# The mixer's linears take x times its weight, with 1/rms applied where VectorE reads them out

## The reference, cut to what matters

```python
xn = rms_norm(h, ln1_g)                 # x / sqrt(mean(x*x) + 1e-6) * gain
proj = xn @ w_in                        # columns: u_s5, q, k, v, gate_logits
gates = sigmoid(gate_logits + b_gate)   # g_s5, g_attn
y_s5 = s5_mixer(u_s5, ...) @ w_s5_branch
y_attn = sliding_window_attention(rms_norm(q), rms_norm(k), v, ...) @ w_attn_branch
h = h + (g_s5 * y_s5 + g_attn * y_attn) @ w_out
h = h + peer_mixer(rms_norm(h, ln2_g), ...)
```

## Time and profile before

| | us |
|---|---|
| median of 3 runs | 4320.23 |
| lowest and highest | 4318.43, 4323.8 |
| the profiled execution | 4325.75 |
| its span, first to last instruction | 4323.9 |

### The profile page before, as it was taken

One profiled execution on the slowest core, in us unless ns is written; L12 is line 12 of the kernel. 1 busy time (PEld: TensorE's weight loads), 2 busy tenths in 40 slices (PEclk: granted clock), 3 DMA queues, 4 the chain that ended last, 5 costly groups with the idle time before them and its releaser, 6 DMA issues.

```text
span 4323.9 us, 50161 instructions
## 1 busy us (share of the span) xinstructions
PE 3998.2 (92%) x15912; PEld 2782.1 (64%) x15912; DVE 2172.7 (50%) x4235; ACT 1290.0 (30%) x2792; POOL 2264.6 (52%) x2979
## 2 busy tenths in 40 slices
PE   8999987778777777999999999999999999999998
PEld 6777633333333333688867767888888867768887
DVE  8466786776777775432154544331332165534322
ACT  2132322222222222422223433332332133323222
POOL 6655633333333333566655445665665745536664
PEclk9999999999999999999999999999999999999999
DMA  6331699999999999423222112323223212213232
GB/s 161 85 113 67 261 427 427 427 427 427 425 427 427 414 427 427 162 95 97 93 71 71 62 62 79 106 96 99 94 97 95 97 55 69 78 46 109 95 96 82
DMA packets 182757, 807.79 MB, mean 187 GB/s; under 512 B 40544, under 2 KB 45072, under 8 KB 117008
## 3 DMA queue, kind: packets, MB, share of 16 engines
q0 software_dynamic: 73728, 536.90, 29.5%
q1 hardware_dynamic: 79936, 256.76, 18.1%
q10 hardware_dynamic: 28880, 11.54, 1.4%
HBM read 796.87 MB, written 7.34 MB: 186 GB/s over the span
## 4 chain that ended last, share of the span: by engine, by line
PE 62%; DMA 15%; DVE 9%; issue 5%; POOL 5%; ACT 2%; DVEq 1%; ACTq 0%; POOLq 0%; SPq 0%
PE bank L771 16%; PE bank L773 15%; PE bank L772 15%; DMA rows_w<-in_peer_uv,expert 5%; PE bank L1176 5%; DMA rows_o<-in_peer_uv,expert 5%; POOL wl L644 5%; DMA rows_x<-in_peer_uv,expert 3%; DMA work<-in_peer_uv,expert 1%; DVE rows_w L2403 1%; PE bank L860 1%; DVE rows_o L2403 1%; DVE rows_x L2403 1%; PE bank L1217 1%; PE bank L1349 1%
## 5 line engine op out<-in xcount | busy, mean ns | idle before, releaser
L644 POOL TENSOR_TENSOR wl<-raw,wh 128x256 fp32r<-128x256 f32 (+1 forms) x1928 | 1515.1, 815 | 645.4 <-ACT wh L1744 605.3
L771 PE MATMUL bank<-xh,wh 128*128 128x512 f32 x2304 | 918.7, 399 | 3.5 <-POOL wl L644 1.9
L773 PE MATMUL bank<-xh,wl 128*128 128x512 f32 x2304 | 900.4, 391 | 0.0
L772 PE MATMUL bank<-xl,wh 128*128 128x512 f32 x2304 | 899.2, 390 | 0.0
L771 PEld LDWEIGHTS bank<-xh,wh 128*128 128x128 f32 x2304 | 433.6, 188 | 133.3 <-issue 35.8
L1744 ACT ACTIVATE wh<-raw 128x1024 fp32r<-128x1024 f32 x296 | 312.2, 1056 | 693.3 <-PE bank L773 570.0
L773 PEld LDWEIGHTS bank<-xh,wl 128*128 128x128 f32 x2304 | 433.6, 188 | 92.4
L772 PEld LDWEIGHTS bank<-xl,wh 128*128 128x128 f32 x2304 | 434.2, 188 | 87.2 <-issue 1.9
L2449 DVE TENSOR_TENSOR work<-bank,rstd 128x512 f32<-128x512 f32 x176 | 121.3, 691 | 537.8 <-PE bank L773 536.3
L1176 PE MATMUL bank<-rows_w,diag 128*128 128x512 f32 x624 | 314.0, 653 | 82.1 <-ACT diag L1708 82.1
L1176 PE MATMUL bank<-rows_o,diag 128*128 128x512 f32 x640 | 308.1, 630 | 69.2 <-ACT diag L1708 69.2
(11 more groups left out here) (473 smaller groups left out, 6015.0 us busy)
## 6 DMA issues: line engine op xcount, KB each, us to landing
raw<-in_w_l SPq DMA_DIRECT2D x316, 512.0 KB, 3.2
raw<-in_w_l SPq DMA_DIRECT2D x64, 448.0 KB, 3.3
raw<-in_w SPq DMA_DIRECT2D x54, 512.0 KB, 3.2
raw<-in_w_l SPq DMA_DIRECT2D x56, 256.0 KB, 2.6
raw<-in_w SPq DMA_DIRECT2D x20, 256.0 KB, 2.6
bias_scratch<-work ACTq DMA_DIRECT2D x1, 3072.0 KB, 33.1
raw<-in_uq_l SPq DMA_DIRECT2D x8, 384.0 KB, 3.0
rows_o<-in_peer_uv,expert POOLq DMA_INDIRECT x160, 19.5
```

The lines of the kernel that those rows point to most:

```text
L644: last = gp.tensor_tensor(wl[:, slot, c], raw[:, rslot, c], f32(wh[:, slot, c]), ALU.subtract)
L771: pe.matmul(bank[b][:], wh[:, slot, c], ah, start=k == 0, stop=False)
L772: pe.matmul(bank[b][:], wh[:, slot, c], al, start=False, stop=False)
L773: mm = pe.matmul(bank[b][:], wl[:, slot, c], ah, start=False, stop=k == last)
```

## The change

- x is no longer normalised before the linears. ACT writes `xh` = round(x * gain) straight from x, DVE writes `xl` = x * gain - xh, and neither waits for `rstd`.
- The squares use three buffers. PE adds four before linear u0 and four behind it; ACT then makes `rstd`, which stays in its tile until the end of the attention.
- 1/rms is applied when a linear is read: by DVE, as bank * rstd, for u (four), k, v (two each), gate_s and gate_a (eight each), where ACT read them before. ACT's tanh then works on the stored tile. q is read unscaled by ACT; its own norm takes eps * rms * rms as epsilon instead (`q_eps`, from four small PE products of `rstd`), and its square root is four instructions instead of one.
- SP loads the second half of x behind the first weight tile.
- The phase tables come from two ACT sines over 128x1024 of an angle that DVE makes in five instructions, in place of the doublings and widenings.
- On DVE the powers of C stand before the turned inputs and the scan. The readouts of k stand before the scan, those of v and gate_s behind the states.
- On PE the lag matrices stand two to a k-step within q3 (i = 3), and wait for one copy of the turned powers rather than eight; the second four turns follow q3; `steps_in` runs whole after i = 5. On ACT the eight `u_step` loads and the bias DMA stand behind q1's readout, where they stood behind q0's.
- In the attention ACT copies the odd transpose between the exps of its two items, not after both.

```diff
 
 
-TURN_AFTER, LAGS_WITH, IN_WITH, OUT_WITH = (2, 3), (4, 5), 6, (15, 16, 17)
+TURN_AFTER, LAGS_WITH, IN_AFTER, SHIFT_AFTER, OUT_WITH = (2, 3), 3, 5, (5, 6), (15, 16, 17)
 
...
             sp.dma_start(c1[:], d["cols1"]).then_inc(c1_loaded, 16)
-            for n in range(2):
+
+            def load_x(n):
+
                 half = slice(n * KD // 2, (n + 1) * KD // 2)
                 sp.dma_start(x[:, half, :], d["xT"].rearrange("(k p) t -> p k t", p=P)[:, half, :]).then_inc(x_loaded[n], 16)
...
-
+                        if stage == "u" and j == 0:
+                            load_x(1)
+
+            load_x(0)
             stage1("u", "w8_1")
...
-            norm(KD, None)
-            ready = normed_ready()
-            first_two(AT_1["u"], None, ready)
-            for j in range(2, 4):
+            def add_square(k):
+
+                pe.wait_ge(sq_ready.sem, sq_ready.at(use.next("sq"), None))
+                mm = pe.matmul(total[:], ones[:], square_tile[k % 3], start=k == 0, stop=k == KD - 1)
+                mm.then_inc((sq_used if k < KD - 1 else summed).sem, 1)
+
+            wait_total(None)
+            for k in range(4):
+                add_square(k)
+            linear(AT_1["u"], 0, None, normed, normed_ready())
+            for k in range(4, KD):
+                add_square(k)
+            for j in range(1, 4):
                 linear(AT_1["u"], j, None, normed)
...
-            pe.matmul(turn[0:HEADS1, 0:3 * P], tabs[:, 0:HEADS1], tabs[:, HEADS1:], start=True, stop=True).then_inc(turned.sem, 1)
+            pe.matmul(turn[0:HEADS1, 0:3 * P], tabs[:, 0:HEADS1], tabs[:, HEADS1:], start=True, stop=True)
+            pe.wait_ge(total_read.sem, total_read.at(1, None))
+            for tb in range(NB):
+                mm = pe.matmul(turn[:, 3 * P + tb:3 * P + tb + 1], rstd[:, tb * P:(tb + 1) * P], ident[:, 0:1], start=True, stop=True)
+            mm.then_inc(turned.sem, 1)
...
                 ri, q = divmod(n, 4)
                 if n >= 4:
-                    pe.wait_ge(s5_copied, n - 3)
+                    pe.wait_ge(s5_copied, max(4, n - 2))
                 for t in range(4 * q, 4 * q + 4):
-                    mm = pe.transpose(four[n % 4][:, t % 4 * P:(t % 4 + 1) * P],
+                    mm = pe.transpose(turn_banks[n][:, t % 4 * P:(t % 4 + 1) * P],
...
-                    pe.wait_ge(s5_copied, 8)
+                    pe.wait_ge(s5_copied, 1)
...
-                if i in LAGS_WITH:
+                if i == LAGS_WITH:
                     for n in range(KD):
                         linear(AT_1[stage], jj, None, normed, share=(n, KD))
-                        lag_matrix(LAGS_WITH.index(i) * KD + n)
-                elif i == IN_WITH:
-                    for half in range(2):
-                        steps_in(half)
-                        linear(AT_1[stage], jj, None, normed, share=(half, 2))
+                        lag_matrix(2 * n)
+                        lag_matrix(2 * n + 1)
                 elif i in OUT_WITH:
...
+                if i == IN_AFTER:
+                    steps_in(0)
+                    steps_in(1)
...
+            def raw_high(k):
+
+                act.wait_ge(x_loaded[k // (KD // 2)], 16)
+                act.activation(xh[:, k, :], x[:, k, :], ACT.Copy, scale=c1[:, C1["ln1"] + k:C1["ln1"] + k + 1]).then_inc(hi_ready.sem, 1)
+
+            def raw_square(k):
+
+                if k >= 3:
+                    act.wait_ge(sq_used.sem, k - 2)
+                act.activation(square_tile[k % 3], x[:, k, :], ACT.Square).then_inc(sq_ready.sem, 1)
+
+            for k in range(4):
+                raw_high(k)
+                raw_square(k)
+            scan_turns()
+            for k in range(4, KD):
+                raw_high(k)
+            for k in range(4, KD):
+                raw_square(k)
+            root(None)
...
+            def store_inputs(j):
 
                 act.wait_ge(*read_at(AT_1["u"], j, None))
                 act.dma_start(d["u_scratch"][j * P:(j + 1) * P, :], u1[:, j, :]).then_inc(s5_u_out, 16)
 
+            for j in range(3):
+                store_inputs(j)
             act.wait_ge(loaded, LOADS)
-            act.wait_ge(xn_ready.sem, xn_ready.at(KD, None))
-            act.activation(c_neg, c_im[:], ACT.Copy, scale=-1.0).then_inc(s5_neg, 1)
+            act.activation(c_neg, c_neg, ACT.Copy, scale=-1.0).then_inc(s5_neg, 1)
...
+            def start_turns():
+
+                act.wait_ge(s5_sin, 3)
+                act.activation(start_s[:], angle[:], ACT.Sin, scale=-6.283185)
+                act.activation(start_c[:], start_c[:], ACT.Sin, bias=quarter[:], scale=-6.283185).then_inc(s5_act, 1)
+
...
-                if i == 0:
+                if i == 1:
+                    store_inputs(3)
                     load_steps()
                     act.wait_ge(brow_ready, 1)
                     act.dma_start(d["bias_rows"].rearrange("h (q m) -> h q m", q=P),
@@ -1588,8 +1584,10 @@
                     act.wait_ge(s5_neg, 1)
                     for n in range(4):
                         copy_powers(4 * TURN_AFTER.index(i) + n)
-                if i == IN_WITH:
-                    shift_lags()
+                    if i == TURN_AFTER[0]:
+                        start_turns()
+                if i in SHIFT_AFTER:
+                    shift_lags(SHIFT_AFTER.index(i))
...
+                for qb in range(NB):
+                    c = slice(HEADS1 * qb, HEADS1 * (qb + 1))
+                    ins = act.activation(q_rms[:, c], score[0][:, c], ACT.Sqrt, bias=q_eps[:, qb:qb + 1], scale=1.0 / 64)
+                ins.then_inc(qk_root, 1)
...
-            for j in range(pairs + 5):
-                if 4 <= j < pairs + 4:
-                    i = j - 4
+            def copy_probs(i):
+
+                if 0 <= i < pairs:
                     lo = (1 - item_1(i)[1]) * P
                     copy_turn(pt1[:, i % 2, lo:T], None, turn[:, lo:T])
+
+            for j in range(pairs + 5):
+                if j % 2 == 0 or j >= pairs:
+                    copy_probs(j - 4)
                 if j < pairs and j % 2 == 0:
                     act.wait_ge(max_ready.sem, max_ready.at(j // 2 + 1, None))
                     for i in (j, j + 1):
+                        if i > j:
+                            copy_probs(j - 3)
                         h, g = item_1(i)
                         c = 2 * (i % 4)
...
+                if j >= 8 and j % 4 == 0:
+                    m = (j - 8) // 4
+                    gate("gate_a", m, gate1[:, m, :], cs[:, 8 + m:9 + m])
...
+            for k in range(KD):
+                dve.wait_ge(hi_ready.sem, hi_ready.at(use.next("xn"), None))
+                dve.scalar_tensor_tensor(xl[:, k, :], x[:, k, :], c1[:, C1["ln1"] + k:C1["ln1"] + k + 1], f32(xh[:, k, :]),
+                                         ALU.mult, ALU.subtract).then_inc(xn_ready.sem, 1)
...
+            def read_inputs(j):
+
+                readout(AT_1["u"], j, None, lambda ps: dve.tensor_tensor(u1[:, j, :].rearrange("p (a n) -> p a n", a=LAG), by_lag(ps),
+                                                                          by_lag(rstd[:]), ALU.mult))
...
             for k, (a_, b_, c_) in enumerate(((6, 7, 8), (4, 6, 8), (0, 4, 8))):
+                if k == 0:
+                    dve.wait_ge(total_read.sem, total_read.at(use.next("total"), None))
+                read_inputs(k)
                 grow(k, lags(b_pow, b_, c_), lags(b_pow, a_, b_), 16 * (b_ - a_), (grow_a, grow_b), (ALU.subtract, ALU.add))
             dve.memset(stat[:, 62:63], 0.0).then_inc(s5_powers, 1)
+            read_inputs(3)
 
             dve.wait_ge(loaded, LOADS)
             dve.wait_ge(turned.sem, turned.at(use.next("turn"), None))
-            dve.tensor_tensor(brow, turn[0:HEADS1, 0:3 * P], nmask[:], ALU.add).then_inc(turn_read.sem, 1)
+            dve.tensor_tensor(brow, turn[0:HEADS1, 0:3 * P], nmask[:], ALU.add)
+            dve.reciprocal(q_eps[:], turn[:, 3 * P:3 * P + NB]).then_inc(turn_read.sem, 1)
+            settle()
+            dve.tensor_tensor(q_eps[:], q_eps[:], q_eps[:], ALU.mult)
+            settle()
+            dve.tensor_scalar(q_eps[:], q_eps[:], EPS, None, ALU.mult)
...
             dve.memset(stat[:, 62:63], 0.0).then_inc(brow_ready, 1)
 
-            dve.tensor_copy(turns[:, 0, 0, :], s5v("cos"))
-            dve.tensor_copy(turns[:, 1, 0, :], s5v("sin"))
-            settle()
-            for k in range(8):
...
+            dve.wait_ge(s5_steps, 1)
+            dve.tensor_scalar(kk, s5v("r"), LAG / TURN, None, ALU.mult)
+            settle()
+            wide = [P, S5_TILES, STEPS]
+            dve.tensor_tensor(angle[:], kk.unsqueeze(2).to_broadcast(wide), steps[:].unsqueeze(1).to_broadcast(wide), ALU.mult)
+            settle()
+            dve.tensor_scalar(start_c[:], angle[:], MAGIC, None, ALU.add)
+            settle()
+            dve.scalar_tensor_tensor(angle[:], start_c[:], -MAGIC, angle[:], ALU.add, ALU.subtract)
+            settle()
```

(73 more changed lines are left out.)

133 lines of the change are left out of this document (32 added, 101 removed).

## The result

The changed kernel takes 4327.56 us (median of 20, 4322.27 to 4330.49), the kernel before beside it 4318.77 (20 runs, 4313.36 to 4327.76): a ratio of 1.0017 [1.001, 1.0023]. In a second round it was 4326.86 against 4323.34, 1.0005 [0.9996, 1.0014]. So it is no change to slightly slower, where 11.8 us (0.27%) faster was forecast. The profiled executions are 4326.32 (span 4324.5) and 4325.75: that of the kernel before lay 7.0 us above its median of these 20 runs, that of the changed kernel 1.2 under its own. Of the 19.2 us between the forecast median (4308.4) and the measured one, 12.4 can be read between the two profiled executions; the other 6.8 lie in the step from them to the medians.

What follows compares the result with a forecast made beforehand. PE, busy 92%, was taken as the bound, so only its waits and lowered clock counted. 10.0 - 0.7 + 2.5 = 11.8 us off 4325.75 gave 4313.9, or 4308.4 as a median, range 4297 to 4318.

Steps and rivals of the forecast that it cites:

- the start: First linears: PE starts u0 at about 13 instead of 24.7; DVE, setting the rest, is 8 us earlier.
- the new stall: Inside q3: PE idles about 4.6 to 5 us for ACT's first copy, then loses clock; steps in end at 102.1.
- from 55.9 this ends at 64.6: ACT's line before q3's wait: u3 store, landing, eight loads, bias DMA, q2's readout and first copy, done at 64.6.
- I take 7.5, the nearest row: Clock loss behind q3's idle, between 0 and 7.5 us, taken as 7.5 from 16.6 us at 0.50 in the steps out.
- the old stall: PE's wait for the powers of C: steps out end at 187.8 instead of 197.8, 10.0 us gained.
- the 1.0 for g2: PE's wait for v0's bank at g2, between 0 and 3.1 us, taken as 1.0.
- The -0.7 at v's transposes: g7 is read by DVE, then tanh, before ACT copies v's transposes: PE waits 0.6 longer, counted as -0.7.
- so I take +2.5: Attention: net gain of 2.5 us from ACT's earlier copy against eight DVE readouts of 0.69.
- The bounds (-6.2 to +6): Attention: +6 if nearly all waits go, -6.2 if each readout lengthens its pair by 0.77.
- rival 3: Attention gets longer as DVE's readouts delay scores without slack: gain 3.1, 4317 us; chance 0.14.
- The rule on the ports: Two-SBUF-input DVE instructions lock out GpSimd's SBUF reads, one-input ones do not: readouts cost 0.69, `c_pow` stays as slow.

Runs made afterwards that it cites:

- late start: copies first, with 14 more squares on ScalarE before its first high half, so the first linear starts later: 4320.36 us, 10.9 slower than copies first.
- copies first, powers of C as before: copies first, with VectorE making `c_pow` behind the states again: 4333.70 us, 24.2 slower than copies first.
- copies first: Changed kernel with ScalarE's eight u loads and bias store moved behind q2's readout and the first four power copies: 4309.45 us, ratio 0.9973 to the kernel before.
- gates by ScalarE: Changed kernel with the attention's gates read by ScalarE's tanh straight from the bank, leaving out gate_a's 1/rms: 4315.98 us, ratio 0.9988 to the kernel before.

## Why the prediction was wrong

**Right: the start.** PE's first linear at 14.1 (13 forecast), q2 done at 58.1 (57), `s5_powers` at 56.3 (55), the last u readout done at 57.5 (55.9). The late start cost 10.9 us for 9.4, part of it by a longer wait in the steps in.

**Right in kind, mis-sized: the new stall.** The step "from 55.9 this ends at 64.6" failed: first copy at 68.2, done at 68.9, with 8.1 us of idle for 4.6 to 5. Two terms were short: the last u readout 1.6 us later (1.0 of it because the four strided readouts took 1.15 each, not 0.9), and the eight loads at 7.38 us, where the earlier trace rows had 4.32. In the changed kernel, a weight load of 512 KB was issued 0.6 us ahead of them; whether that slows them was not tried. In the other kernels that issue the eight together they took between 4.2 and 7.3 us.

**Failed: "I take 7.5, the nearest row" for the clock.** It fell, but for 27.1 us of PE's work (30.7 in all) and not 16.6. Steps in ended at 110.4, not 102.1; 4.3 of these 8.3 us are the late copy, so the clock took 4.0 more than the 7.5, some 11.5. The row taken was one where PE's work behind the idle is the steps out. The forecast compared the two sections by their share of linears, 46 against 42%, and called them alike. What stands behind an idle was the point: 30.7 us at half clock with lag matrices behind 8.1 of idle, 23.9 behind 3.7, 3.4 with turns behind 4.6, and none in the same lag section without an idle. Why the lag matrices hold the clock down and the turns do not is not shown.

**Right: the old stall.** The 4.9 us of wait are gone and the steps out ran at full clock, as forecast. There was no wait at g2, where 1.0 had been taken: `c_pow` took 24.8 us, not 34.1. The steps out ended 2.9 us earlier instead of 10.0; the 7.1 are the stall and clock above, less the 1.0 for g2. The -0.7 at v's transposes was -0.8.

**Failed: "so I take +2.5" in the attention.** It was -3.2, and -1.9 more behind its end. The sum had no clock term there: 13.65 us at half clock, 9.7 in the attention's tail and 4.0 behind it. The bounds (-6.2 to +6) held the -3.2 and rival 3 named VectorE, but both priced a readout by its 0.69 us only. The copies alone were worth +6.5, a little over the +6. With the readouts added, GpSimd's cast began 0.5 us ahead of VectorE's scalings, which then took 2.35 us; holding the cast back gave 10.7 us of attention. That meeting was the missing term.

**The rule on the ports.** The forecast used it for operations with two SBUF inputs. The traces agree there: the `c_pow` block took 34.1 us with POOL busy 32.7 of it (before), 31.5 with 23.8 (copies first, powers of C as before), 24.8 with 14.7 (changed), and 21.2 with 6.3 (copies first). First the kernel before, then the changed one:

```profile
121.70:155.90 34.20, 28.85 (x126) 23.57 (x126) 33.45 (x32) 3.27 (x5) 32.74 (x30) 1.00 0.28 92
```

```profile
95.20:120.00 24.80, 24.80 (x219) 20.77 (x219) 24.11 (x30) 2.38 (x4) 14.72 (x13) 0.98 0.52 101
```

What the forecast passed over is the same section's other half: by the Trainium skill (SBUF — State Buffer, "Who interferes with whom") a `tensor_scalar` may enter a mode that takes the shared pair too, and whoever issues first holds it for its whole instruction. The scalings are `tensor_scalar`, in SBUF alone. No view shows the mode, but the times agree with the rule: 1.01 us for four with the cast behind them, 2.35 with the cast ahead. The readouts of a bank took 1.15 us strided by lag (0.69 to about 1.1 had been the bounds, 0.9 the value taken) and 0.69 plain, as forecast.

```profile
30.41 1.15 DVE L2036 TENSOR_TENSOR u<-bank,rstd 128x512 f32<-128x512 f32 x1
...
132.41 0.69 DVE L2156 TENSOR_TENSOR q<-bank,rstd 128x512 f32<-128x512 f32 x1 [1.92 <-PE bank L782]
```

**The sum.** Against the profiled execution, 4313.9 was forecast and 4326.3 came: 7.1 to the steps out, 0.1 at v, 5.7 in the attention, 1.9 behind it, and 2.4 back later (the lag of 2.9 at 466 us is 0.6 at the end of the span, for no reason found). The step to a median took 5.5 us off that the changed kernel did not give.

## What to carry to other kernels

A change that brings an engine forward moves it onto the next queue: list what stands ahead of the first thing it will wait for (here ten DMA issues on ScalarE), and put the releases first. Price an idle of PE by what PE does behind it: here 3.7 us of idle ahead of the lag matrices meant 23.9 us at half clock, and 4.6 us ahead of the turns meant 3.4. Where VectorE sets the pace, look at which of its instructions GpSimd's next tile will meet; here one wait on the idle engine was worth as much as taking 5.5 us of work off the busy one.

## What the hardware showed

- In q3, ahead of the lag matrices, an idle of 3.7 us on PE went with 23.9 us at 1.2 GHz and one of 8.1 with 30.7; idles of 4.6 and 2.3 us ahead of turns went with 3.4 each. The lag section without an idle ran at 2.4 GHz in 12.1 us; at 1.2 GHz it took 22.8.
- One GpSimd cast of 1.04 us and its subtractions, begun 0.5 us ahead of four 128x128 and 128x256 scalings, made these 2.35 us instead of 1.01; begun in their middle (with the gates by ScalarE: scalings from 307.08, cast from 307.59), 1.79.
- Eight DMA issues of 128 KB on ScalarE took 4.32 us in the kernel before, 7.38 in the changed one and 4.2 to 7.3 in the others.
